# Inversion levels of the Rwkv chunks: the second group of heads on the other half of the PSUM partitions

## The reference, cut to what matters

```
def _rwkv7_step(state, inp):
    r_t, w_t, k_t, v_t, a_t, b_t = inp
    sa = einsum('bhvk,bhk->bhv', state, a_t)
    state = state * w_t + sa[..., None] * b_t + v_t[..., None] * k_t
    y_t = einsum('bhvk,bhk->bhv', state, r_t)
    return state, y_t
```

## Time and profile before

| what | value |
|---|---|
| median of 3 runs | 1446.33 us (1446.31 to 1447.34) |
| the profiled execution | 1446.07 us, of which the profile's span is 1444.3 us |
| the chunks' levels | from 928.6 us to 1043.2 us of the span |
| TensorE clock granted | 1.00 in every stretch |
| ScalarE, VectorE, GpSimd busy over the span | 44%, 44%, 53% |
| mean busy in 945 to 965 us, of 20 us | PE 19.65, DVE 7.31, ACT 8.76, POOL 10.44 |

### The profile page before, as it was taken

How to read it: one execution, slowest core, us unless ns; L and a number is a source line. 1 busy time by engine, 2 the same in 40 slices (tenths; PEclk the granted TensorE clock), 3 DMA queues, 4 the chain that set the end, 5 groups by cost and what they waited for, 6 DMA issues and landing times.

```text
span 1444.3 us, 23375 instructions
## 1 busy us (share of the span) xinstructions
PE 1428.7 (99%) x9196; PEld 1182.5 (82%) x9196; DVE 635.6 (44%) x797; ACT 642.5 (44%) x1097; POOL 763.0 (53%) x609
## 2 busy tenths in 40 slices
PE   9999999999999999999999999999999999999998
PEld 6888887777779888888888887888878878888887
DVE  5566565552246433333635956333345453111122
ACT  6555555454346444444322567434344333222343
POOL 4444343354255766666655647854337655444563
PEclk9999999999999999999999999999999999999999
DMA  5222222221140232232333222200013322232222
GB/s 211 96 76 88 74 87 74 73 102 59 59 146 30 88 102 94 95 102 90 110 107 102 88 74 75 72 3 3 3 59 117 102 88 97 93 103 92 97 99 76
DMA packets 34215, 122.96 MB, mean 85 GB/s; under 512 B 3792, under 2 KB 4304, under 8 KB 34000
## 3 DMA queue, kind: packets, MB, share of 16 engines
q1 hardware_dynamic: 33408, 119.51, 24.4%
q10 hardware_dynamic: 720, 2.20, 0.4%
HBM read 119.59 MB, written 2.10 MB: 84 GB/s over the span
## 4 chain that ended last, share of the span: by engine, by line
PE 92%; DVE 4%; ACT 1%; POOL 1%; DMA 1%; issue 1%; SPq 0%; ACTq 0%; POOLq 0%; DVEq 0%
PE ps L550 19%; PE ps L552 18%; PE ps L551 18%; PE ps L1265 2%; PE ps L1294 2%; PE ps L1296 2%; PE ps L1295 2%; PE ps L1370 2%; PE ps L1372 2%; PE ps L1371 2%; PE ps L1251 1%; PE ps L657 1%; PE ps L672 1%; PE ps L685 1%; PE ps L1087 1%; PE ps L915 1%
## 5 line engine op out<-in xcount | busy, mean ns | idle before, releaser
L2004 POOL TENSOR_TENSOR w_lo<-stage,w_hi 128x512 fp32r<-128x512 f32 x422 | 590.3, 1422 | 508.0 <-ACT w_hi L1401 507.9
L550 PE MATMUL ps<-x_hi,w_lo 128*128 128x512 f32 x888 | 350.7, 395 | 0.0
L552 PE MATMUL ps<-x_hi,w_hi 128*128 128x512 f32 x888 | 346.1, 390 | 0.0
L551 PE MATMUL ps<-x_lo,w_hi 128*128 128x512 f32 x888 | 345.9, 390 | 0.0
L1401 ACT ACTIVATE w_hi<-stage 128x512 fp32r<-128x512 f32 x422 | 241.5, 622 | 63.8 <-DMA stage<-w 56.2
L550 PEld LDWEIGHTS ps<-x_hi,w_lo 128*128 128x128 f32 x888 | 166.8, 188 | 36.6 <-issue 1.7
L551 PEld LDWEIGHTS ps<-x_lo,w_hi 128*128 128x128 f32 x888 | 166.9, 188 | 34.9 <-issue 1.7
L552 PEld LDWEIGHTS ps<-x_hi,w_hi 128*128 128x128 f32 x888 | 166.7, 188 | 35.0
L2477 DVE SCALAR_TENSOR_TENSOR conv<-ps,vcol,conv 128x511 f32<-128x511 f32 x44 | 33.0, 749 | 132.3 <-ACT conv L1619 132.3
L1619 ACT ACTIVATE conv<-ps,vcol 128x512 f32<-128x512 f32 x44 | 34.2, 778 | 121.1 <-PE ps L552 120.2
L2798 DVE TENSOR_TENSOR bt<-gates,ps 128x512 f32<-128x512 f32 x24 | 16.3, 679 | 142.2 <-PE ps L1372 142.2
(11 more groups left out here) (454 smaller groups left out, 2863.7 us busy)
## 6 DMA issues: line engine op xcount, KB each, us to landing
stage<-w SPq DMA_DIRECT2D x211, 512.0 KB, 3.2
extra_stage<-w SPq DMA_DIRECT2D x6, 512.0 KB, 4.9
H<-xT SPq DMA_DIRECT2D x4, 512.0 KB, 7.7
mem<-memT SPq DMA_DIRECT2D x2, 512.0 KB, 11.1
pool_n<-pool_count ACTq DMA_DIRECT2D x1, 1024.0 KB, 6.2
outT<-outs SPq DMA_DIRECT2D x4, 256.0 KB, 2.0
outT<-outs SPq DMA_DIRECT2D x2, 384.0 KB, 2.7
w_small<-small ACTq DMA_DIRECT2D x1, 512.0 KB, 6.0
```

The costliest lines, as they stand in the source:

```text
L550: pe.matmul(out, wl, hi(k), start=first, stop=False)
L551: pe.matmul(out, wh, lo(k), start=False, stop=False)
L552: mm = pe.matmul(out, wh, hi(k), start=False, stop=end)
L2004: pool.tensor_tensor(unit_lo(b)[:, cols], unit_stage(b)[:, cols], unit_hi(b)[:, cols].bitcast(F32), ALU.subtract).then_inc(wlo_made, 1)
```

## The change

The products of group 1 write to the other half of the PSUM partitions: block d of group g goes to half d XOR g. They still read their operands on half d. With this the four kinds of product (g, d) use four different 64x64 tiles of the array. The products of the two groups alternate in TensorE's list, and TensorE waits for both groups ahead of R and ahead of XY. The halves of group 1 are put back in the copies out of PSUM: ScalarE's copy of R for g = 1 and VectorE's update for g = 1 are two instructions of 64 partitions each, which read one half and write the other. Nothing else moves.

```diff
@@ TensorE, level(c, l)
                 before_copies(c, l)
-                for g in range(2):
-                    pe.wait_ge(ch_mk_s, idx + g + 1)
-                    if l == 1:
-                        pe.wait_ge(ch_x0_s, 2 * c + g + 1)
-                    else:
-                        pe.wait_ge(ch_xt_s, idx + g - 1)
+                pe.wait_ge(ch_mk_s, idx + 2)
+                if l == 1:
+                    pe.wait_ge(ch_x0_s, 2 * c + 2)
+                else:
+                    pe.wait_ge(ch_xt_s, idx)
+                for h in range(4):
+                    for g in range(2):
+                        for d in range(2):
+                            mm = pe.matmul(ps[half(d ^ g), g, h * HB:(h + 1) * HB], Mk[half(d), 4 * g + h, :],
+                                           XT[half(d), c % 2, g, 0, h, :], start=True, stop=True)
+                        if h == 3:
+                            mm.then_inc(ch_r_s, 1)
+                beside_copies(c, l)
+                pe.wait_ge(ch_rb_s, idx + 2)
...
+                for part in range(2):
                     for h in range(4):
-                        for d in range(2):
-                            mm = pe.matmul(ps[half(d), g, h * HB:(h + 1) * HB], Mk[half(d), 4 * g + h, :],
-                                           XT[half(d), c % 2, g, 0, h, :], start=True, stop=True)
-                    mm.then_inc(ch_r_s, 1)
-                beside_copies(c, l)
-                for g in range(2):
-                    pe.wait_ge(ch_rb_s, idx + g + 1)
...
-                    for part in range(2):
-                        for h in range(4):
+                        for g in range(2):
                             for d in range(2):
                                 R, T = R1[half(d), g, h, :], XT[half(d), c % 2, g, 1, h, :]
-                                mm = pe.matmul(ps[half(d), 2 + g, (4 * part + h) * HB:(4 * part + h + 1) * HB],
+                                mm = pe.matmul(ps[half(d ^ g), 2 + g, (4 * part + h) * HB:(4 * part + h + 1) * HB],
                                                R if part else T, T if part else R, start=True, stop=True)
-                    mm.then_inc(ch_xy_s, 1)
+                            if part and h == 3:
+                                mm.then_inc(ch_xy_s, 1)
@@ ScalarE
-                        act.activation(R1[:, g, :, :], blocks(g, 0, 4 * HB), ACT.Copy).then_inc(ch_rb_s, 1)
+                        if g == 0:
+                            act.activation(R1[:, 0, :, :], blocks(0, 0, 4 * HB), ACT.Copy).then_inc(ch_rb_s, 1)
+                        else:
+                            act.activation(R1[0:HB, 1, :, :], blocks(1, 0, 4 * HB)[HB:P], ACT.Copy)
+                            act.activation(R1[HB:P, 1, :, :], blocks(1, 0, 4 * HB)[0:HB], ACT.Copy).then_inc(ch_rb_s, 1)
@@ VectorE, update(c, l, g)
+                XT_g = XT[:, c % 2, g, :, :, :]
+                halves = [(slice(0, HB), slice(HB, P)), (slice(HB, P), slice(0, HB))] if g else [(slice(0, P), slice(0, P))]
                 if l < NL:
-                    dve.tensor_tensor(XT[:, c % 2, g, :, :, :].rearrange("p a h n -> p (a h n)"),
-                                      XT[:, c % 2, g, :, :, :].rearrange("p a h n -> p (a h n)"),
-                                      ps[:, 2 + g, :], ALU.add).then_inc(ch_xt_s, 1)
+                    for rows, from_rows in halves:
+                        ins = dve.tensor_tensor(XT_g[rows].rearrange("p a h n -> p (a h n)"),
+                                                XT_g[rows].rearrange("p a h n -> p (a h n)"), ps[from_rows, 2 + g, :], ALU.add)
+                    ins.then_inc(ch_xt_s, 1)
                     return
-                dve.tensor_tensor(XT[:, c % 2, g, 0, :, :], XT[:, c % 2, g, 0, :, :], got[:, 0, :, :], ALU.add).then_inc(ch_xt_s, 1)
+                for rows, from_rows in halves:
+                    ins = dve.tensor_tensor(XT_g[rows, 0], XT_g[rows, 0], got[from_rows, 0, :, :], ALU.add)
+                ins.then_inc(ch_xt_s, 1)
...
                 for d in range(2):
-                    rows = slice(HB * d, HB * d + HB)
-                    ins = dve.tensor_tensor(TF[rows, 4 * g:4 * g + 4, HB * d:HB * d + HB], XT[rows, c % 2, g, 1, :, :],
-                                            got[rows, 1, :, :], ALU.add)
+                    rows, e = slice(HB * d, HB * d + HB), d ^ g
+                    ins = dve.tensor_tensor(TF[rows, 4 * g:4 * g + 4, HB * d:HB * d + HB], XT_g[rows, 1],
+                                            got[HB * e:HB * e + HB, 1, :, :], ALU.add)
```

More of the change, by code:

```diff
@@ L1263, in level @@
+                if l == 1 and c:
+                    pe.wait_ge(ch_tf_s, 2 * c)
+                if l == 1 and c == 0:
+                    pe.wait_ge(rw_shifted_s, 17)
+                for part in range(2):
+                    for h in range(4):
+                        for g in range(2):
                             for d in range(2):
                                 R, T = R1[half(d), g, h, :], XT[half(d), c % 2, g, 1, h, :]
-                                mm = pe.matmul(ps[half(d), 2 + g, (4 * part + h) * HB:(4 * part + h + 1) * HB],
+                                mm = pe.matmul(ps[half(d ^ g), 2 + g, (4 * part + h) * HB:(4 * part + h + 1) * HB],
```

## The result

The changed kernel takes 1471.59 us (median, 1471.14 to 1472.08) against 1446.84 us: ratio 1.0171, 95% interval [1.0159, 1.0183], 24.8 us slower. The forecast was 1454.5 us, slower by 8.2: the right side, inside the range of 1449 to 1475, and a third of the size. One execution of all that follow, of the kernel of experiment 7, took 1468.70 us at a granted clock of 0.927, where the other ten took 1443.3 to 1444.7; its ratio leaves it out.

What follows compares the result with a forecast made beforehand. TensorE, busy 99% of the span, was taken as the bound. With 28 us of array time counted as saved, R to XY gave -4.3 us and XY to R +12.5: +8.2 us, so 1454.5 us, range 1449 to 1475.

Steps and rivals of the forecast that it cites:

- rival A: Instruction stream, not array, sets the pace in R and XY: at 29 ns per product 1482 us; chance 0.16 with D.
- sign of being wrong: Adds of 64x512 not 0.69 us, four tiles at 25 ns or more, or levels not growing 6 to 10 us.
- Array time: R and XY on four tiles: a product every 14.6 ns, by itself saving 28 us over 20 levels.
- D: TensorE starts products in order, a tile's next waiting for the others: 29 ns; chance inside the 0.16 of rival A.
- XY to R, 3.45 us: With nothing before R, three VectorE adds make this step 3.45 us against 2.02; seven places, +10.0 us.
- Rival B: Half an instruction costs half: a 64x512 add at 0.35 us, giving 1442 us; chance 0.05.
- R to XY, 1.78 us: With nothing beside, three ScalarE copies make this step 1.78 us against 1.42; four places, +1.4 us.
- `sa_product`: R to XY with this work beside it: 3.00 to 2.77 us, three places, -0.7 us.
- `state_product`: R to XY with this work and `turn` beside it: 3.62 to 3.16 us, three places, -1.4 us.
- `y_product`: XY to R with this work: 3.91 to 3.45 us, -0.5; third and fourth chunk 4.84 to 3.85, -2.0 us.
- costed at nothing: Masks, earlier semaphore order, `lower`, copies of scores and everything behind the levels: taken to add no time.
- six kinds with a minus sign: Steps forecast to shorten: `turn` alone, `sa_product`, `state_product` with `turn`, one `chunk_scores`, two of them (-2.8 us), `y_product`.

Runs made afterwards that it cites:

- experiment 7: run 5 with four tiles in R alone, XY everywhere straight and in sequence; 1443.68 us, ratio 0.9983.
- run 2: The filler of run 1 thinned out: two products where there were five, one where there were two or three; 1456.56 us, ratio 1.0067.
- run 1: The filled kernel: the changed kernel plus 62 products nobody reads, placed where TensorE stands idle; 1457.04 us, ratio 1.0071.
- run 3: The changed kernel with every product back on its own half, two tiles and whole copies, groups still alternating; 1466.58 us, ratio 1.0130.
- run 5: The kernel before, with joint four-tile R or XY only at chosen places where other TensorE work hides the copies; 1442.19 us, ratio 0.9965.
- run 6: run 5 with joint four-tile R also in every level 1 and in level 2 of chunks 2 to 4; 1439.66 us, ratio 0.9955.
- run 4: The changed kernel in the old order, group 0 then group 1 with own waits, group 1 still crossed with halved copies; 1452.51 us, ratio 1.0039.

## Why the prediction was wrong in size

The forecast's range held by luck. Its upper part was there for rival A, slower tiles, and that is not what happened; a cause that the forecast does not name took the time into it. Its own sign of being wrong did come: the levels' stretch was to grow by 6 to 10 us and grew by 25.8. Term by term:

- **Array time: right.** 14.6 ns for four tiles; R and XY at 0.48 and 0.94 us from first to last start. Rival A falls, and D with it. The Trainium skill's 25 ns floor ("TensorE: Matmul & The Clock Gate", Part 1, "Wait — 56ns, not 53.3ns?") does not hold here: 64 MATMUL start within 0.94 us, 15 ns each, with weight loads between.
- **XY to R, 3.45 us: right.** Measured 3.44 to 3.45, the three adds 2.10 us; `corner_first` after 3.41 (3.40 forecast). Rival B falls: 64x512 costs 0.69.
- **R to XY, 1.78 us: mis-sized.** Measured 1.95. I let the copies overlap by 0.1 us; they stand 0.41 and 0.39 us apart and end 1.90 us after R starts, just past the 1.86 that I named for that case. XY starts 0.05 us behind them, where I had taken 0.14, the wait behind an add. Ten places, 1.7 us.
- **`sa_product`: better.** 2.55 us instead of 2.77, three times, -0.7; `state_product`, 3.17 and 3.35 after 3.62 and 3.80, gains 0.45 each time, as forecast. `y_product` of the third and fourth chunk, 3.85, is as forecast too, but it took 4.78 before and not the 4.84 that I had worked out, so each gain is 0.93.
- **The sum at full clock:** 8.2 + 1.7 - 0.7 - 0.2 (the last chunk's end, 3.32 us, before 3.58) = 9.0. The filled kernel measures 9.7 over before, 0.7 of it the filler's overrun, and the two executions of run 2 at a clock of 1.00 measure 9.0 and 9.3 over theirs.
- **The step that failed: the clock.** The forecast has TensorE idle about 2.2 us ahead of each R, says that "behind the added waits of TensorE stands only its own next work", and prices that work at its old pace, with the clock left at 1.00 as every row of before shows it. It lists what is "costed at nothing", and the clock is not even among it. Place by place against the filled kernel: R to XY of level 5 4.17 for 2.55, three times (4.9 us); `y_product` 6.15 and 6.19 for 3.85 (4.6) and 4.27 for 3.45 (0.8); the first chunk's levels 2 and 3, 4.27 for 3.45 twice and one R to XY 2.38 for 1.95 (2.1); `sa_product` up to 3.42 for 2.55 (1.9); the last chunk's levels 4 and 5 with the conv products behind them (2.2): 16.5 us, two thirds of the result. Most of it falls on steps that were forecast as gains: in level 5, -0.93 us became +0.70.

That the idle time let the clock fall is shown by run 1, where filling it kept the clock at 1.00, and runs 2 and 3 agree with it. How much idleness it takes stays open. Run 2 says only that a part of the filler was enough in two of four executions and nearly so in the others, and that the time then scatters by 4 us; TensorE's longest idle time there is 1.3 us, against 2.3 in the changed kernel.

## What to carry to other kernels

Where two groups alternate through one engine and its copies, ending them together to fill the array trades hidden copies for visible ones; do it only where that engine has other work to put there. Count the idle time that a faster step leaves, and before believing the sum ask whether TensorE keeps its full clock: a stretch at half clock charges the work beside it too. A list of places with signs is worth more than its total: four of its six kinds with a minus sign turned +24.8 into -5.1 us (run 5), and the steps measured there, which the list could not give, led on to -6.7 (run 6). Joint R in level 5, the list's largest gain in R to XY, was not tried by itself.

## What the runs showed of the hardware

- Instructions that change the half of the partitions they read do not overlap with the one ahead: whole adds stand 0.60 us apart (1.28 us for two, run 3), crossed ones 0.70 (2.10 for three); on ScalarE 0.28 against 0.40. The Trainium skill has the rule for VectorE ("VectorE: DVE Perf Modes", "Two Vector instructions with no wait between them": an instruction whose input starts in another quadrant than the last is held until the earlier ones end) and the traces agree; for ScalarE the traces alone show it.
- TensorE starts a matmul on a free tile ahead of older ones that wait for theirs, across groups (run 4): XY of a level with other work beside it takes 1.69 us from first to last start instead of 1.86, the next group's start on the other tiles hiding 0.17 us.
- From 1004 to 1010 us the clock is at 0.50 with TensorE busy all the time, while it was 0.99 in the stretch before with 3.97 of 6 us: here the penalty comes after the idle time, on dense work.
